# Differential attention's scores as three single-pass products of split queries and keys

## The reference

```python
def attend(q, k, v, lam):
    s = jnp.einsum('bhmqd,bhmkd->bhmqk', q, k, preferred_element_type=jnp.float32) * (B_QK ** -0.5)
    p = jax.nn.softmax(s, axis=-1)
    w = p[:, :, 0] - lam * p[:, :, 1]
    return jnp.einsum('bhqk,bhkv->bhqv', w.astype(v.dtype), v)
```

## Time and profile before

| | us |
|---|---|
| median of 3 runs | 2349.66 |
| lowest and highest run | 2343.83, 2352.79 |
| the profiled execution's own time | 2347.91 |
| its span in the profile | 2346.1 |
| TensorE busy, of the span | 2250.4 |
| VectorE, ScalarE, GpSimd busy | 1213.5, 1119.3, 729.2 |

### The profile page before, as it was taken

One profiled execution on the slowest core, in us unless ns is written; L12 is line 12 of the kernel. 1 busy time (PEld: TensorE's weight loads), 2 busy tenths in 40 slices (PEclk: granted clock), 3 DMA queues, 4 the chain that ended last, 5 costly groups with the idle time before them and its releaser, 6 DMA issues.

```text
span 2346.1 us, 41405 instructions
## 1 busy us (share of the span) xinstructions
PE 2250.4 (96%) x14956; PEld 1940.0 (83%) x14956; DVE 1213.5 (52%) x2183; ACT 1119.3 (48%) x2323; POOL 729.2 (31%) x563
## 2 busy tenths in 40 slices
PE   7989999989999899999999999999989999999998
PEld 4858899867899798878879669888879999787998
DVE  3765434686335644551243765354456564437563
ACT  3554454555445534542354663233334565647553
POOL 2504464422555321112222002222213225221443
PEclk9989999999999999999999999999999999999999
DMA  8667966656876332112222112222223335222554
GB/s 298 227 217 232 305 192 218 209 191 238 284 252 190 120 103 72 63 63 92 88 73 89 38 37 81 89 72 96 92 71 121 100 105 175 85 84 70 163 162 142
DMA packets 159787, 328.58 MB, mean 140 GB/s; under 512 B 17696, under 2 KB 21024, under 8 KB 159520
## 3 DMA queue, kind: packets, MB, share of 16 engines
q1 hardware_dynamic: 159504, 325.80, 42.6%
q0 software_dynamic: 144, 0.85, 0.1%
HBM read 325.53 MB, written 1.05 MB: 139 GB/s over the span
## 4 chain that ended last, share of the span: by engine, by line
PE 65%; issue 18%; POOL 8%; DVE 4%; ACT 2%; DMA 2%; SPq 1%; POOLq 0%; DVEq 0%; ACTq 0%
PE PS L1795 13%; PE PS L1797 13%; PE PS L1796 13%; POOL WL L1712 6%; PE PS L1840 4%; PE PS L1842 4%; PE PS L1841 4%; PE PS L690 2%; PE PS L670 1%; POOL AR L1732 1%; DMA RAW<-stream 1%; PE PS L704 1%; PE PS L706 1%; PE PS L705 1%; DMA WORK<-mods 1%
## 5 line engine op out<-in xcount | busy, mean ns | idle before, releaser
L1712 POOL TENSOR_TENSOR WL<-RAW,WH 128x512 fp32r<-128x512 f32 x468 | 653.1, 1397 | 1545.4 <-ACT WH L2102 1393.8
L1795 PE MATMUL PS<-AR,WH 128*128 128x256 f32 (+1 forms) x2632 | 860.3, 327 | 3.2 <-DVE AR L1575 2.0
L1797 PE MATMUL PS<-AR,WL 128*128 128x256 f32 (+1 forms) x2632 | 843.8, 321 | 0.0
L1796 PE MATMUL PS<-AR,WH 128*128 128x256 f32 (+1 forms) x2632 | 843.7, 321 | 0.0
L2102 ACT ACTIVATE WH<-RAW 128x512 fp32r<-128x512 f32 x908 | 535.8, 627 | 399.9 <-DMA RAW<-stream 200.9
L2360 DVE TENSOR_TENSOR WL<-RAW,WH 128x512 fp32r<-128x512 f32 x468 | 399.4, 853 | 568.0 <-ACT WH L2102 566.4
L1795 PEld LDWEIGHTS PS<-AR,WH 128*128 128x128 f32 x2632 | 496.4, 189 | 77.0 <-issue 25.7
L1796 PEld LDWEIGHTS PS<-AR,WH 128*128 128x128 f32 x2632 | 496.6, 189 | 41.2 <-issue 2.4
L1797 PEld LDWEIGHTS PS<-AR,WL 128*128 128x128 f32 x2632 | 496.2, 189 | 40.1
L1840 PE MATMUL PS<-WH,AR 128*128 128x256 f32 x768 | 219.4, 286 | 0.5 <-issue 0.5
L1842 PE MATMUL PS<-WH,AR 128*128 128x256 f32 x768 | 216.3, 282 | 0.0
(11 more groups left out here) (301 smaller groups left out, 2920.7 us busy)
## 6 DMA issues: line engine op xcount, KB each, us to landing
RAW<-stream SPq DMA_DIRECT2D x936, 256.0 KB, 3.0
WORK<-mods SPq DMA_DIRECT2D x144, 512.0 KB, 6.4
C<-consts SPq DMA_DIRECT2D x1, 1088.0 KB, 7.4
XX<-xT SPq DMA_DIRECT2D x1, 1024.0 KB, 10.5
XX<-ctxT SPq DMA_DIRECT2D x1, 1024.0 KB, 5.9
outT<-XX SPq DMA_DIRECT2D x1, 1024.0 KB, 4.8
C<-consts POOLq DMA_DIRECT2D x1, 832.0 KB, 6.9
WORK<-lam SPq DMA_DIRECT2D x1, 256.0 KB, 7.9
```

The lines of the kernel that those rows point to most:

```text
L1712: pool.tensor_tensor(WL[:, u % 4, cut, :], RAW[:, (2 * u + 1) % 4, :, :], WH[:, u % 4, cut, :].bitcast(f32), ALU.subtract).then_inc(lo_don ...
L1795: pe.matmul(out, WH[:, u % 4, k, :], moving[:, 0, k, :], start=(k == 0), stop=False)
L1796: pe.matmul(out, WH[:, u % 4, k, :], moving[:, 1, k, :], start=False, stop=False)
L1797: last = pe.matmul(out, WL[:, u % 4, k, :], moving[:, 0, k, :], start=False, stop=(k == KC - 1))
```

## The change

Keys and queries of differential attention are split as the weights are: after the rotation ScalarE copies each key chunk into `KHI` (`key_high`), and VectorE subtracts to get `KLO` (`key_low`); the same for the queries with `query_high` and `query_low`, where `QHI` holds four heads at a time and `QLO` overwrites `YB`. `score` makes three single-pass products for each map instead of one f32 product, and waits for `kq_lo` too. All 8 key chunks and the first 4 query heads are split among the projections of keys and values; heads 4 to 7 of the queries within the attention loop, ScalarE's part at the end of each of the first four heads, after `exps`, and VectorE's a step later. `KHI` and `KLO` lie where `Y2` is; so gated z moves from there to `KB`, which nothing reads once the keys are split. Two semaphores that nothing used are renamed.

```diff
--- before.py
+++ after.py
@@ -253,11 +253,13 @@
     SG, SZ = work(20480, 2, 2 * T), work(21504, 2, 2 * T)
     SQB, RB = work(16384, 2, 2 * T), work(17408, 2, 2 * T)
     TC, TS = work(18432, 2, T), work(18944, 2, T)
+    KHI, KLO = (AR[:, at:at + 4096].rearrange("p (k t) -> p k t", k=KC) for at in (8192, 12288))
+    QHI, QLO = work(17408, 4, 2 * T, of=WR), work(0, KC, 2 * T, of=WR)
     PB, WT = work(19456, 2, 2, 2 * T), work(21504, 2, 4, P)
     YS = work(21504, 2, 2 * T)
     FOLD, SINES = work(17408, 4, T), work(18432, 4, 2, P)
     VP = work(19456, 2, 2 * T)
-    SZ2 = work(12288, KC, 2 * T, of=ARF)
+    SZ2 = KB
     SQH = work(16384, 2, 2 * T)
     LAM, LT = work(11264, DEPTH, 4, 64), work(11776, 2, DEPTH, 64)
 
@@ -283,8 +285,8 @@
     stats_done, qs_read, qs_done, band_done, sel_done = (
         sem(n) for n in ("stats_done", "qs_read", "qs_done", "band_done", "sel_done"))
     index_done, index_read, stick_read = sem("index_done"), sem("index_read"), sem("stick_read")
-    sticks, wk_done = sem("sticks"), sem("wk_done")
-    ffg = sem("ffg")
+    sticks, kq_hi = sem("sticks"), sem("kq_hi")
+    kq_lo = sem("kq_lo")
     rot_done, cosd, rot_read = sem("rot_done"), sem("cosd"), sem("rot_read")
     rope_done = sem("rope_done")
     scores, masked, exped = sem("scores"), sem("masked"), sem("exped")
@@ -665,10 +667,14 @@
                 keys = 2 * T if q >= 2 else T
                 if f >= 2:
                     pe.wait_ge(ex2, tile_base(l) + f - 1)
-                for m in range(2):
-                    rows = slice(64 * m, 64 * m + 64)
-                    last = pe.matmul(PS[:, 2 * (f % 2) + m, 0:keys], YB[rows, h, q * P:(q + 1) * P],
-                                     KB[rows, h, 0:keys], start=True, stop=True)
+                pe.wait_ge(kq_lo, 16 * l + 8 + h + 1)
+                own = slice(q * P, (q + 1) * P)
+                for x, (still, moving) in enumerate(((QHI[:, h % 4, own], KHI), (QHI[:, h % 4, own], KLO),
+                                                     (QLO[:, h, own], KHI))):
+                    for m in range(2):
+                        rows = slice(64 * m, 64 * m + 64)
+                        last = pe.matmul(PS[:, 2 * (f % 2) + m, 0:keys], still[rows, :], moving[rows, h, 0:keys],
+                                         start=(x == 0), stop=(x == 2))
                 last.then_inc(s2, 1)
 
             def turn(f):
@@ -1022,6 +1028,19 @@
                 inverse_root(RB[:, x % 2, :], VP[:, x % 2, :], PS[:, 4 + x % 2, :], 1.0 / 64,
                              (prs, 8 * l + x + 1), prx, YS[:, x % 2, :])
 
+            def key_high(x):
+
+                act.wait_ge(p_done, 16 * l + 8 + x + 1)
+                act.activation(KHI[:, x, :], KB[:, x, :], ACT.Copy).then_inc(kq_hi, 1)
+
+            def query_high(h):
+
+                if h < 4:
+                    act.wait_ge(p_done, 16 * (l + 1))
+                else:
+                    act.wait_ge(s2, tile_base(l) + per_head(l) * (h - 3))
+                act.activation(QHI[:, h % 4, t0:], YB[:, h, t0:], ACT.Copy).then_inc(kq_hi, 1)
+
             for x in range(8):
                 projected(st["bq"], x, YB, t0, "qn", x)
             for x in range(8):
@@ -1032,12 +1051,19 @@
                                  (q2_read, l + 1), q2_root)
                 else:
                     key_roots(x - 1)
+                if x >= 3:
+                    key_high(x - 3)
             for j in range(4):
                 act.wait_ge(bank_read[(st["bv"] + j) % 4], earlier(st["bv"] + j))
             key_roots(7)
+            key_high(5)
             take = values(st["bv"])
             for j in range(8):
                 take(j)
+                if j < 2:
+                    key_high(6 + j)
+                elif j < 6:
+                    query_high(j - 2)
             gate_functions()
             steps, tb, per = tiles(l), tile_base(l), per_head(l)
 
@@ -1085,6 +1111,8 @@
                                ACT.Copy).then_inc(wt2, 1)
                 if f + 2 < len(steps):
                     exps(f + 2)
+                if f % per == per - 1 and f // per < 4:
+                    query_high(f // per + 4)
                 for x in ended(f, l):
                     z_unit(x)
                 for half in range(2):
@@ -1416,6 +1444,17 @@
                 refine(RB[:, x % 2, :], VP[:, x % 2, :], YS[:, x % 2, :])
                 dve.tensor_tensor(KB[:, x, :], KB[:, x, :], RB[:, x % 2, :], ALU.mult).then_inc(pscaled, 1)
 
+            def key_low(x):
+
+                dve.wait_ge(kq_hi, 16 * l + x + 1)
+                dve.tensor_tensor(KLO[:, x, :], KB[:, x, :], KHI[:, x, :].bitcast(f32), ALU.subtract).then_inc(kq_lo, 1)
+
+            def query_low(h):
+
+                dve.wait_ge(kq_hi, 16 * l + 8 + h + 1)
+                dve.tensor_tensor(QLO[:, h, t0:], YB[:, h, t0:], QHI[:, h % 4, t0:].bitcast(f32),
+                                  ALU.subtract).then_inc(kq_lo, 1)
+
             for x in range(8):
                 next_low(st["bq"], 0, x)
                 if x:
@@ -1432,13 +1471,21 @@
                     rotated(8 + x - 2)
                 if x:
                     key_norm(x - 1)
+                if x >= 4:
+                    key_low(x - 4)
             key_norm(7)
             rotated(14)
             for j in range(2):
                 next_low(st["bv"], 0, j)
             rotated(15)
+            key_low(4)
             for j in range(2, 8):
                 next_low(st["bv"], 0, j)
+                if j < 5:
+                    key_low(j + 3)
+                else:
+                    query_low(j - 5)
+            query_low(3)
             steps, tb, per = tiles(l), tile_base(l), per_head(l)
 
             def top(f):
@@ -1507,6 +1554,8 @@
                     z_unit(x)
                 for x in ended(-1, l) if f == 0 else ended_since(f, 2 - l, l):
                     next_low(st["bz"], 0, x)
+                if f and f % per == 0 and f // per <= 4:
+                    query_low(f // per + 3)
                 for h in summed(f, l):
                     head_sum(h)
             for f in range(len(steps), len(steps) + per + 3):
```

## The result

| | before | after |
|---|---|---|
| median, us | 2348.62 (20 runs) | 2352.26 (20 runs) |
| lowest and highest | 2342.25, 2352.79 | 2346.79, 2359.50 |
| profiled span, us | 2346.1 | 2349.6 |

The ratio is 1.0019, with a 95% interval of 1.0011 to 1.0028: slower by 2.6 to 6.6 us. That is far inside the 0.5% that the prediction called no change, but it is clear of noise, and the forecast of 2.8 us faster has the wrong sign. The forecast of 2346.9 us stood on a median of three runs, 2349.66; with 20 runs that median is 2348.62.

What follows compares the result with a forecast made beforehand. TensorE was taken to bound nearly every stage. Scores −5.7, start of attention +2.6 and loop +0.3 summed to −2.8 us, giving 2346.9 us from a median of 2349.66; the range was 2336 to 2358.

Steps and rivals of the forecast that it cites:

- What a score costs: Attention scores: 1.06 us with 512 keys and 0.64 with 256 now, 0.90 and 0.57 afterwards.
- c: Fixed part of a score, about 0.21 us, read as the first weights' load and emptying the array.
- All three rivals on that point: Scores: maps not side by side (2374, chance 0.13); weights not loaded behind (2356, 0.13); fixed 0.21 us gone (2337, 0.06).
- two-pass execution: Rival at the scores: the half-height fp32r product is done in two passes, 19 us more, 2369; chance 0.03.
- So the loop goes at TensorE's pace, and time taken off a score comes off the stage: First layer's attention: TensorE sets the pace, so score savings count in full, except in 4 tiles.
- The prediction had 5.7: Gain in us from shorter scores in both attentions: 6.2 less 0.5 for four pairs ending behind a wait.
- Within the loop ... I take 0.3 us: Attention loops: 4 copies and 4 differences added per layer cost 0.3 us, ScalarE and VectorE having time to spare.
- the bounds of 0 and 7.9: Lower and upper bound, in us, for the cost of copies and differences added within the attention loops.
- The fourth rival: Attention loop: VectorE or ScalarE becomes the bound, +4.8 us in all, 2354; chance 0.06.
- Splitting in the projections costs nothing: Before attention: ScalarE's added copies and VectorE's differences cost zero, TensorE being full, except the last ones.
- The start: Start of attention: last query differences delay the first maxima, costing 1.0 us in the first layer, 1.6 in the second.
- that of the plain durations, 0.9: Start of attention: the cost in us without the rule that VectorE and GpSimd block each other, in place of 2.6.

Runs made afterwards that it cites:

- e9: Against e8, the second layer's weights' subtraction also moved, to between combine and the next maxima; median 2342.59 us, ratio to before 0.9967.
- e1: Against the kernel after, only the three products kept, all query and key splits and their waits removed; median 2342.57 us, ratio to before 0.9984.
- e3: Against the kernel after, copies and differences of query heads 4 to 7 in the loop removed; median 2344.02 us, ratio to before 0.9994.
- e6: Against the kernel after, only the loop's four query differences moved, to between combine and the maxima; median 2351.49 us, ratio to before 1.0012.
- e10: The kernel after, unchanged, profiled once more on another execution; 2351.26 us (one run), both attentions 189.20 us.
- e4: Against the kernel after, the query differences of both start and loop moved, as e5 and e6 do singly; median 2343.66 us, ratio to before 0.9997.
- e8: Against e4, ScalarE's query copy of heads 4 to 7 made a step earlier in the first layer; median 2343.16 us, ratio to before 0.9977.
- e7: Against the kernel after, one map's three products issued before the other's three; median 2355.02 us (5 runs), ratio to before 1.0036.
- e5: Against the kernel after, only the differences of query heads 0 to 3 moved, into VectorE's idle time in the values' units; median 2344.49 us, ratio 0.9991.
- e2: Against the kernel after, all splitting and its waits kept but scores made by plain f32 products; median 2354.03 us, ratio to before 1.0034.

## Why the prediction was wrong, point by point

- **What a score costs: right.** c of 0.21 us and a pass of 0.23 gave 0.90 and 0.57; measured 0.90 and 0.56. Maps run side by side, weights load behind a pass. All three rivals on that point are out, and so is two-pass execution: six records for a tile, not more.
- **"So the loop goes at TensorE's pace, and time taken off a score comes off the stage": the first failed step.** It was argued from views of TensorE that show no wait. They show none because VectorE's chain was as long as TensorE's work, within 0.12 us of 8.13 (e9). Of 6.2 us, e1 shows 3.75 coming off. The prediction had 5.7.
- **"Within the loop ... I take 0.3 us": the step that turned the sign.** I read the idle time of VectorE (29.1 us of waits) as room for work anywhere. It lies between `combine` and the next maxima; the new work was put between the maxima and `combine`. The prediction names what is queued behind it as `z_unit` and ScalarE's copy of the transposed weights; on VectorE it is the next `combine`, for which TensorE waits. Measured 3.1 us (e3), within the bounds of 0 and 7.9. The fourth rival, VectorE the bound in the loop with +4.8 in all, is the mechanism that happened, and it had 0.06. It was stated as an engine running out of time; VectorE is busy 23.3 of 28 us and is still the bound.
- **The clock: not in the sum at all.** At the first layer's start the kernel before runs at a mean clock of 0.83 (1290 to 1300 us) and after at 1.00, which gives back 1.3 us, and a fall in the third head takes 1.5. The net is small, but 1.5 us is half of what was forecast. That the later start is what removed the first fall isn't shown: e6 starts as late and has it.
- **Splitting in the projections costs nothing: right**, though `key_low` took 1.10 us on average and not 0.69. From the first product of `key_sums` to the first score is 92.0 us before and 92.1 after, in both layers.

**The start: mechanism right, size a little low.** 1.30 and 1.89 us later at the third score against 1.0 and 1.6. VectorE and GpSimd at the start of the first layer:

```profile
1282.30 1.28 POOL L1761 TENSOR_TENSOR WL<-RAW,WH 128x512 fp32r<-128x512 f32 x1 [7.80 <-ACT WH L2151]
1282.34 1.78 DVE L1455 TENSOR_TENSOR WR<-WORK,WR 128x512 fp32r<-128x512 f32 x1
...
1283.82 1.46 POOL L1761 TENSOR_TENSOR WL<-RAW,WH 128x512 fp32r<-128x512 f32 x1 [0.24 <-ACT WH L2151]
...
1284.05 1.78 DVE L2409 TENSOR_TENSOR WL<-RAW,WH 128x512 fp32r<-128x512 f32 x1
...
1285.75 1.28 DVE L1455 TENSOR_TENSOR WR<-WORK,WR 128x512 fp32r<-128x512 f32 x2
...
1286.96 0.68 DVE L1496 TENSOR_REDUCE BC<-PS 128x2 f32<-128x512 f32 x1
```

`query_low(1)` takes 1.78 us beside GpSimd's subtraction, the weights' subtraction behind it 1.78 beside the next, and the last two differences, with GpSimd done, 1.28 together, or 0.64 each. The estimate of 2.6 us, against 3.2 measured, was better than that of the plain durations, 0.9. The Trainium skill's page SBUF — State Buffer (summary: rules for kernel authors) says that a VectorE operation with two SBUF inputs and a GpSimd operation that reads SBUF don't run together: the second to issue is blocked until the first finishes. The trace agrees: `query_low(1)` takes 1.10 us longer beside a GpSimd subtraction of 1.28 us. I had missed that `query_low(1)` would be caught first and pass its delay on.

**The sum as it should have been:** products −3.75, loop +3.1, start +3.2 less 1.3 for the clock, third head's clock +1.5: +2.8, against +3.0 measured in e10 and +3.8 in after, which has a further fall of 0.8 us in the second layer.

## What to carry to other kernels

Where one engine shows no wait, it may still be level with a chain through another: follow the time from a result's end through every instruction in front of the one that the bound engine needs next, and compare the two lengths before you credit a saving. Extra work for an engine with idle time must be put into the idle time, by the instruction in front of which that engine waits, and its operand must be ready by then (e4 against e8: the same slot, 0.55 us a head apart). Here 0.4 us of work cost 0.33 behind the maxima and nothing in front of them, right behind `combine`.

## What the runs showed of the hardware that I had not expected

- Products on the upper and the lower 64 rows run side by side even when the program issues the three of one half in a row ahead of the three of the other: 0.91 us for six products of 512 columns (e7) against 0.90 when they alternate.
- A two-operand subtraction of VectorE takes 1.78 us instead of 0.68 for 512 columns beside one of GpSimd's, and 1.51 instead of 0.41 for 256 (three of `query_low` in after's second layer). Each one that meets a further subtraction of GpSimd pays again: 1.78 and 1.78 in a row at the first layer's start, a delay that a single price doesn't cover.
- TensorE's clock falls to the lower level (1.2 GHz) for 3.4 or 6.8 us inside the attentions. One such fall costs 1.3 to 1.5 us in the first layer and 0.4 to 0.8 in the second. In the first layer all kernels with an early start (4.6 to 4.8 us: before, e1, e4, e5, e8, e9) have one there, and of those with a late one (6.0 to 6.1: after, e10, e2, e3, e6, e7) only e6. A fall later on comes in the third head in after, e10 and e9, and in head 6 (14.44 to 14.48 us instead of 12.99) in e4 to e7; e2 and e3 have none in this layer. So its place goes with the order of the work, but no run shows what sets it. In the second layer after, e2, e3 and e6 have one, and the same program has none in e10.
